# The rotary columns of latent attention: one 128-column product for the swapped queries, one pass for the key's two parts

## The chip, the cores and the metric

The program runs on one core of one Trainium2 chip. The metric is the time of one execution on the device in microseconds (us), first to last instruction and what lies around them. Smaller is better.

## What is computed

Two layers of a hybrid block over 256 latent tokens and 256 context tokens of width 1024: a modulated norm, one input projection, four parallel groups of token mixing, an output projection, and a mixture of 16 experts. The change lies in group D, the multi-head latent attention with rotary position parts:

```python
MLA_HEADS, MLA_Q_RANK, MLA_KV_RANK = 4, 256, 128
MLA_NOPE_DIM, MLA_ROPE_DIM = 64, 32

def rope_2d(x, cos, sin):
    r1, r2, c1, c2 = jnp.split(x, 4, axis=-1)
    x1 = jnp.concatenate([r1, c1], axis=-1)
    x2 = jnp.concatenate([r2, c2], axis=-1)
    o1 = x1 * cos - x2 * sin
    o2 = x1 * sin + x2 * cos
    ...

pl = modulate(rms_norm(xl, norm1_g[l]), mod_l[0], mod_l[1]) @ w_in[l]      # latent tokens; pc likewise for context
dl, dc = pl[..., OFF_D:], pc[..., OFF_D:]
q = (rms_norm(dl[..., :256], gq) @ w_uq).reshape(B, L, 4, 64 + 32)          # 64 plain, 32 rotary columns a head
k_rope = dl[..., 256 + 128:]                                                # 32 columns, shared by the heads
qr_l, kr_l = rope_2d(qr_l, cos, sin), rope_2d(kr_l, cos, sin)               # latent tokens only
```

A rotation is `x * cos + swapped(x) * sin`, where `swapped` exchanges the halves of each group of 16 columns and the sign stands in `sin`. The kernel takes the swapped vector from the same product as the vector itself, with a second copy of the weight columns in swapped order.

## The kernel before

Activations lie with their features on the 128 partitions and the tokens along a row: `x_t` is 8 chunks of 128 features by 512 tokens (256 latent, 256 context). A large product is done in three passes of TensorE: weights and activations are each split into a high and a low part (`w_hi`, `w_lo`, `h_hi`, `h_lo`), and `product` (L1177 to L1179) adds hi·hi, hi·lo and lo·hi into one PSUM bank. The split of a weight block is a copy on ACT (`w_hi`, L809) followed by a subtraction on DVE (`w_lo`, L1807).

The input projection of a layer runs over eight blocks of 256 weight columns, n = 0 to 7. `W_COLS = [6, 7, 5, 4, 0, 1, 2, 3]` says which columns each takes: n = 0 holds the low-rank query (`q_low`), n = 1 holds the low-rank key and value (128 columns, `kv_low`) and the 32 rotary key columns (`k_rope`), which GpSimd (POOL) follows with a swapped copy of them (`swap`, L664), so that the block is 192 columns wide. A block of features is a pass `by_feature(n, dst, c0, m, width)`: 8 chunks of 3 matmuls, with `m` weight columns from `c0` held still and `width` tokens streamed. After a block come two things in TensorE's program: a product of the modulation, `modulate(q, bank[7])` at L1206 in layer 0 after blocks 2 to 7 and in layer 1 after blocks 3 and 5, and `after_block(n)`, small products that the block before made possible. In the middle of the next block stands `turn(q, bank[7])` (L1214), which waits for `mod_row`, a row that DVE copies from `bank[7]` (`take_rows`, L1828).

For n = 1 TensorE does three passes: 128 columns by 512 tokens into `bank[2]` (`kv_low`), 96 columns by 512 tokens into `bank[3]`, and 96 columns by 256 latent tokens into `bank[4]`. The last two are 96 wide although only 32 columns of each are wanted, so that the rotary columns land on partitions 64 to 95 in the first and the swapped ones on the same partitions in the second. There DVE makes the key's rotation: L1946 (`k_rope`), L1947 (`k_turn`), L1948, L1951, all on `rr`, partitions 64 to 95.

For the queries GpSimd builds `w_uqs` in `small_weights` (L684, L688), each head's 96 columns with the last 32 swapped. After block 6, `after_block(6)` multiplies it: four heads by two chunks, 96 columns by 256 latent tokens each (L1352), two heads to a bank. In plain float32, each such product appears as two matmul records in the profile. Then comes `up_k(0, bank[4])` (L1312), the first half of the keys. DVE turns the result into `rope_t` with the sine (L1989), multiplies `q_mla` by the cosine (L1995) and adds (L1996); only after these, in layer 0, does it reach `take_rows(6)` (L1828), for whose `mod_row` the `turn(6)` inside block 7 waits.

All order is written out by hand: each engine has one program, and semaphores (`used`, `s_up`, `s_rot`, `s_mod`, `split_lo`) tie them. Weight blocks come through a ring of six 1 MB buffers `raw`, loaded in one order on SyncE's queue (SP). A buffer comes free when DVE has made `w_lo` from it, or, for modulation weights, when `modulate` has read it (L594, L535, L548).

Of the kernel before, what the change touches and what calls it, by code (L numbers as in the profile page):

```python
# [84 lines left out]
def constants():  # L85
# [20 lines left out]
    for part in range(2):  # L106
        for half in range(2):
            r = NOPE + part * 2 * nf + half * nf
            c[r:r + nf, C_COS:C_COS + S] = cos[part * nf:(part + 1) * nf]
            c[r:r + nf, C_SIN:C_SIN + S] = sin[part * nf:(part + 1) * nf] * (-1 if half == 0 else 1)  # L110
# [5 lines left out]
def build(nc, a, out):  # L116
    with ExitStack() as ctx:  # L117
# [42 lines left out]
        w_uqs = sb("w_uqs", [P, 2, HEADS, QK])  # L160
# [487 lines left out]
        def _(pool):  # L648
# [18 lines left out]
            def small_weights(l):  # L667
# [15 lines left out]
                for c in range(2):  # L683
                    pool.tensor_copy(w_uqs[:, c, :, 0:NOPE], w4[:, c, :, 0:NOPE])  # L684
                    for half in range(2):
                        for part in range(2):
                            to, fr = NOPE + 16 * part + 8 * half, NOPE + 16 * part + 8 * (1 - half)
                            last = pool.tensor_copy(w_uqs[:, c, :, to:to + 8], w4[:, c, :, fr:fr + 8])  # L688
# [93 lines left out]
        def _(act):  # L782
# [133 lines left out]
            for l in range(DEPTH):  # L916
# [13 lines left out]
                for n in range(N_WIN):  # L930
# [29 lines left out]
                    if n == 4:  # L960
                        for h in range(3):
                            act.wait_ge(s_up, l * 9 + h + 1)
                            act.activation(q_mla[0:QK, h, 0:width], bank[4 + h][0:QK, 0:width], ACT.Copy, scale=MLA_SCALE).then_inc(s_qe, 1)
                    if n == 5:
                        act.wait_ge(s_up, l * 9 + 4)
                        act.activation(q_mla[0:QK, 3, 0:width], bank[4][0:QK, 0:width], ACT.Copy, scale=MLA_SCALE).then_inc(s_qe, 1)
                    if n == 6:
                        act.wait_ge(s_up, l * 9 + 7)
                        act.activation(k_mla[0:NOPE, 0, :], bank[4][0:NOPE, :], ACT.Copy)
                        act.activation(k_mla[0:NOPE, 1, :], bank[4][NOPE:P, :], ACT.Copy).then_inc(s_ke, 1)  # L970
                    if n == 7:
                        act.activation(v_na[:, 0:2, :].rearrange("p t n -> p (t n)"), bank[2][:, :], ACT.Copy).then_inc(proj_ea, 1)
                        act.wait_ge(s_up, l * 9 + 8)
                        act.activation(k_mla[0:NOPE, 2, :], bank[4][0:NOPE, :], ACT.Copy)
                        act.activation(k_mla[0:NOPE, 3, :], bank[4][NOPE:P, :], ACT.Copy).then_inc(s_ke, 1)
                        act.wait_ge(s_up, l * 9 + 9)
# [197 lines left out]
        def _(pe):  # L1174
# [92 lines left out]
            for l in range(DEPTH):  # L1267
# [48 lines left out]
                def after_block(n, l=l):  # L1316
# [31 lines left out]
                    if n == 6:  # L1348
                        pe.wait_ge(s_go, l + 1)
                        for h in range(HEADS):  # L1350
                            for c in range(2):
                                ins = pe.matmul(bank[5 + h // 2][0:QK, (h % 2) * S:(h % 2 + 1) * S], w_uqs[:, c, h, :],  # L1352
                                                q_low[:, c, 0:S], start=(c == 0), stop=(c == 1))
                            if h % 2:
                                ins.then_inc(s_up, 1)
# [13 lines left out]
                for n in range(N_WIN):  # L1369
# [18 lines left out]
                    elif n == 1:  # L1388
                        by_feature(n, bank[2], 0, P, T)
                        by_feature(n, bank[3], 64, QK, T)  # L1390
                        ins = by_feature(n, bank[4], 96, QK, S)
# [400 lines left out]
        def _(dve):  # L1792
# [113 lines left out]
            for l in range(DEPTH):  # L1906
# [29 lines left out]
                for n in range(N_WIN):  # L1936
# [8 lines left out]
                    if n == 1:  # L1945
                        dve.tensor_copy(k_rope[rr, :], bank[3][rr, :])  # L1946
                        then(dve.tensor_tensor(k_turn[rr, :], bank[4][rr, 0:S], const[rr, C_SIN:C_SIN + S], ALU.mult))  # L1947
# [38 lines left out]
                    if n == 6:  # L1986
                        dve.wait_ge(s_up, l * 9 + 6)
                        for h2 in range(2):
                            ins = dve.scalar_tensor_tensor(rope_t[rr, 2 * h2:2 * h2 + 2, :], bank[5 + h2][rr, :].rearrange("p (h t) -> p h t", h=2),  # L1989
                                                           MLA_SCALE, const[rr, C_SIN:C_SIN + S][:, None, :].to_broadcast([ROPE, 2, S]),  # L1990
                                                           ALU.mult, ALU.mult)
# [387 lines left out]
```

## Time and profile before

| | |
|---|---|
| median of 3 executions | 944.04 us (940.52 to 949.8) |
| profiled execution | 942.83 us |
| its span, first to last instruction | 941.0 us |
| mean granted clock of TensorE | 0.935 of full speed |
| PE (matmul) busy | 853.3 us, 91% |
| DVE, ACT, POOL busy | 551.7, 463.5, 77.8 us |
| moved by DMA | 197.50 MB |

PE is TensorE's matmuls and PEld its weight loads. A matmul's duration overlaps the next one's, so what a matmul costs in a stream is the distance from its start to the next start. The input projection of layer 0 lies at about 50 to 189 us, that of layer 1 at about 575 to 669 us.

### The profile page before, as it was taken

Reading aid. Unit: us, or ns where it says so; the run is one execution under the profiler, and the core shown is the slowest. Engines: PE = TensorE matmul, PEld = TensorE weight load, DVE = VectorE, ACT = ScalarE, POOL = GpSimd, SP = SyncE. Lnnn points to the kernel's source line nnn. Section 1 sums busy time; section 2 is a strip of 40 time slices with the busy share of each in tenths; the row PEclk is TensorE's granted clock in tenths of the full one; section 3 lists DMA queues with packets and bytes.
Section 4 is the critical chain, followed back from the end, with each engine's and each line's share of the span. In section 5 each row is a group of like instructions: output and inputs, shape, how many; then the busy total and the mean of one; then the engine's idle time right before and its main releaser. Section 6 shows DMA issues by size and latency. Waiting matters only on the chain. (4 is left out here: it accounts for less than half of the span.)

```text
span 941.0 us, 15302 instructions
## 1 busy us (share of the span) xinstructions
PE 853.3 (91%) x6114; PEld 728.1 (77%) x6114; DVE 551.7 (59%) x800; ACT 463.5 (49%) x637; POOL 77.8 (8%) x107
## 2 busy tenths in 40 slices
PE   3989999999998889999999567999999799999986
PEld 2768867756786689999999466887769599999974
DVE  1263312349534868777777374434285678888853
ACT  2262211168523556655665337422384557776734
POOL 0103000610012000000000132002200100000000
PEclk9799999999999699999999756999999799999996
DMA  9793898793121157888888891279063249999901
GB/s 327 219 311 103 281 320 275 237 311 99 53 90 46 45 175 259 293 293 283 288 293 272 262 280 50 91 227 310 10 215 117 78 134 316 349 339 330 351 20 45
DMA packets 165443, 197.50 MB, mean 210 GB/s; under 512 B 11346, under 2 KB 152572, under 8 KB 165372
## 3 DMA queue, kind: packets, MB, share of 16 engines
q1 hardware_dynamic: 160720, 180.70, 60.2%
q10 hardware_dynamic: 3500, 11.64, 3.2%
q0 software_dynamic: 1152, 4.19, 1.3%
q8 instruction: 47, 0.77, 0.4%
q14 instruction: 24, 0.20, 0.1%
HBM read 187.09 MB, written 9.44 MB: 209 GB/s over the span
## 5 line engine op out<-in xcount | busy, mean ns | idle before, releaser
L2072 DVE TENSOR_TENSOR w_lo<-raw,w_hi 128x2048 fp32r<-128x2048 f32 x96 | 219.5, 2290 | 38.0 <-ACT w_hi L1034 37.4
L1034 ACT ACTIVATE w_hi<-raw 128x2048 fp32r<-128x2048 f32 x96 | 183.5, 1913 | 67.1 <-PE bank L1179 58.1
L1177 PE MATMUL bank<-h_hi,w_hi 128*128 128x512 f32 (+3 forms) x304 | 109.6, 360 | 12.5 <-DVE h_lo L1864 10.4
L1177 PE MATMUL bank<-w_hi,xg_hi 128*128 128x256 f32 x384 | 111.7, 291 | 2.9 <-DVE xg_lo L2233 2.4
L1178 PE MATMUL bank<-w_lo,xg_hi 128*128 128x256 f32 x384 | 109.3, 285 | 0.0
L1179 PE MATMUL bank<-w_hi,xg_lo 128*128 128x256 f32 x384 | 109.2, 284 | 0.0
L1178 PE MATMUL bank<-h_lo,w_hi 128*128 128x512 f32 (+3 forms) x304 | 106.2, 349 | 0.0
L1179 PE MATMUL bank<-h_hi,w_lo 128*128 128x512 f32 (+3 forms) x304 | 106.0, 349 | 0.0
L1177 PEld LDWEIGHTS bank<-w_hi,xg_hi 128*128 128x128 f32 x384 | 74.1, 193 | 3.2 <-issue 3.2
L1177 PEld LDWEIGHTS bank<-h_hi,w_hi 128*128 128x128 f32 (+1 forms) x304 | 57.6, 190 | 23.8 <-issue 9.5
L1178 PEld LDWEIGHTS bank<-w_lo,xg_hi 128*128 128x128 f32 x384 | 74.4, 194 | 0.0
L1179 PEld LDWEIGHTS bank<-w_hi,xg_lo 128*128 128x128 f32 x384 | 74.3, 193 | 0.0
L1807 DVE TENSOR_TENSOR w_lo<-raw,w_hi 128x2048 fp32r<-128x2048 f32 (+1 forms) x20 | 45.1, 2263 | 48.5 <-ACT w_hi L809 48.3
L809 ACT ACTIVATE w_hi<-raw 128x2048 fp32r<-128x2048 f32 (+1 forms) x20 | 37.2, 1867 | 72.1 <-PE bank L1179 26.2
L1596 PE MATMUL bank<-onehot,h_tok 128*128 128x256 f32 x512 | 64.5, 284 | 1.3 <-DVE onehot L2078 1.3
L1596 PEld LDWEIGHTS bank<-onehot,h_tok 128*128 128x128 f32 x512 | 63.5, 192 | 2.3 <-ACT h_tok L881 1.7
L1179 PEld LDWEIGHTS bank<-h_hi,w_lo 128*128 128x128 f32 (+1 forms) x304 | 57.8, 190 | 7.7
L1178 PEld LDWEIGHTS bank<-h_lo,w_hi 128*128 128x128 f32 (+1 forms) x304 | 57.8, 190 | 7.5 <-issue 0.2
L1177 PE MATMUL bank<-w_hi,ht_hi 128*128 128x512 f32 x128 | 52.8, 412 | 6.7 <-DVEq L2336 4.1
L1179 PE MATMUL bank<-w_hi,ht_lo 128*128 128x512 f32 x128 | 52.1, 407 | 0.0
L1178 PE MATMUL bank<-w_lo,ht_hi 128*128 128x512 f32 x128 | 52.0, 406 | 0.0
L1206 PE MATMUL bank<-raw,c_pad 128*32 128x256 f32 x768 | 45.8, 392 | 2.5 <-DMA raw<-in_ada_w 2.5
(292 smaller groups left out, 1619.7 us busy)
## 6 DMA issues: line engine op xcount, KB each, us to landing
raw<-in_ada_w SPq DMA_DIRECT2D x48, 1024.0 KB, 9.9
raw<-in_moe_w_gate SPq DMA_DIRECT2D x32, 1024.0 KB, 6.1
raw<-in_moe_w_up SPq DMA_DIRECT2D x32, 1024.0 KB, 6.5
raw<-in_moe_w_down SPq DMA_DIRECT2D x32, 1024.0 KB, 6.0
raw<-in_w_in SPq DMA_DIRECT2D x14, 1024.0 KB, 9.7
raw<-in_w_out SPq DMA_DIRECT2D x8, 1024.0 KB, 9.7
y_rows<-y_sb ACTq DMA_DIRECT2D x16, 512.0 KB, 5.0
na_bias<-in_na_rpb SPq DMA_DIRECT2D x4, 384.0 KB, 8.3
```

The lines of the kernel that those rows point to most:

```text
L809: act.activation(w_hi[slot][:, :, 0:w], raw[n % RAW][:, :, 0:w], ACT.Copy).then_inc(split_hi, 1)
L1034: act.activation(w_hi[slot][:, :, :], raw[q][:, :, :], ACT.Copy).then_inc(split_hi, 1)
L1177: pe.matmul(dst, w_hi_, x_hi_, start=first, stop=False)
L1178: pe.matmul(dst, w_hi_, x_lo_, start=False, stop=False)
L1179: return pe.matmul(dst, w_lo_, x_hi_, start=False, stop=last)
L1206: ins = pe.matmul(dst[32 * g:32 * g + 32, 0:BW], c_pad[:, k, :], raw[raw_index(l, j) % RAW][:, k, :], start=(k == 0), stop=(k == KC - 1))
L1596: ins = pe.matmul(bank[c // 2][:, (c % 2) * 2 * SLOTS:(c % 2 + 1) * 2 * SLOTS], h_tok[part][:, t, c * P:(c + 1) * P], onehot[:, t, :], sta ...
L1807: dve.tensor_tensor(w_lo[slot][:, :, 0:w], raw[n % RAW][:, :, 0:w], w_hi[slot][:, :, 0:w].bitcast(F32), ALU.subtract).then_inc(split_lo, 1)
L2072: dve.tensor_tensor(w_lo[slot][:, :, :], raw[q][:, :, :], w_hi[slot][:, :, :].bitcast(F32), ALU.subtract).then_inc(split_lo, 1)
```

## The change

The constants `cos` and `sin`, which lay on partitions 64 to 95, are repeated on all four groups of 32 partitions. `w_uqs` keeps only the 32 swapped columns of each head, so that four heads make one stationary operand of 128 columns: `after_block(6)` does one product of two chunks into `bank[5]`, with head h on partitions 32h to 32h+31. DVE then makes `rope_t` in four instructions, one a head, each reading another group of partitions of `bank[5]` and of the sine, and writing partitions 64 to 95. GpSimd no longer copies the plain columns. For n = 1 the two 96-column passes become one pass of 64 columns by 512 tokens into `bank[3]`: rotary columns on partitions 0 to 31, swapped on 32 to 63. DVE reads them there and writes partitions 64 to 95. The counts of `s_up` fall from 9 to 8 a layer. Nothing else is touched.

```diff
@@ constants()
-    for part in range(2):
+    for part in range(2 * P // ROPE):
         for half in range(2):
-            r = NOPE + part * 2 * nf + half * nf
-            c[r:r + nf, C_COS:C_COS + S] = cos[part * nf:(part + 1) * nf]
...
+            r = part * 2 * nf + half * nf
+            c[r:r + nf, C_COS:C_COS + S] = cos[part % 2 * nf:(part % 2 + 1) * nf]
...
-        w_uqs = sb("w_uqs", [P, 2, HEADS, QK])
+        w_uqs = sb("w_uqs", [P, 2, HEADS, ROPE])
@@ small_weights, GpSimd
                 for c in range(2):
-                    pool.tensor_copy(w_uqs[:, c, :, 0:NOPE], w4[:, c, :, 0:NOPE])
                     for half in range(2):
                         for part in range(2):
-                            to, fr = NOPE + 16 * part + 8 * half, NOPE + 16 * part + 8 * (1 - half)
+                            to, fr = 16 * part + 8 * half, NOPE + 16 * part + 8 * (1 - half)
                             last = pool.tensor_copy(w_uqs[:, c, :, to:to + 8], w4[:, c, :, fr:fr + 8])
@@ after_block, TensorE
                     if n == 6:
                         pe.wait_ge(s_go, l + 1)
-                        for h in range(HEADS):
-                            for c in range(2):
-                                ins = pe.matmul(bank[5 + h // 2][0:QK, (h % 2) * S:(h % 2 + 1) * S], w_uqs[:, c, h, :],
-                                                q_low[:, c, 0:S], start=(c == 0), stop=(c == 1))
-                            if h % 2:
-                                ins.then_inc(s_up, 1)
+                        for c in range(2):
+                            ins = pe.matmul(bank[5][:, 0:S], w_uqs[:, c, :, :].rearrange("p h r -> p (h r)"), q_low[:, c, 0:S],
+                                            start=(c == 0), stop=(c == 1))
+                        ins.then_inc(s_up, 1)
@@ block n == 1, TensorE
                         by_feature(n, bank[2], 0, P, T)
-                        by_feature(n, bank[3], 64, QK, T)
-                        ins = by_feature(n, bank[4], 96, QK, S)
+                        ins = by_feature(n, bank[3], P, 2 * ROPE, T)
@@ block n == 1, DVE
-                        dve.tensor_copy(k_rope[rr, :], bank[3][rr, :])
-                        then(dve.tensor_tensor(k_turn[rr, :], bank[4][rr, 0:S], const[rr, C_SIN:C_SIN + S], ALU.mult))
+                        dve.tensor_copy(k_rope[rr, :], bank[3][0:ROPE, :])
+                        then(dve.tensor_tensor(k_turn[rr, :], bank[3][ROPE:2 * ROPE, 0:S], const[ROPE:2 * ROPE, C_SIN:C_SIN + S], ALU.mult))
@@ block n == 6, DVE
-                        dve.wait_ge(s_up, l * 9 + 6)
-                        for h2 in range(2):
-                            ins = dve.scalar_tensor_tensor(rope_t[rr, 2 * h2:2 * h2 + 2, :], bank[5 + h2][rr, :].rearrange("p (h t) -> p h t", h=2),
-                                                           MLA_SCALE, const[rr, C_SIN:C_SIN + S][:, None, :].to_broadcast([ROPE, 2, S]),
+                        dve.wait_ge(s_up, l * 8 + 5)
+                        for h in range(HEADS):
+                            hr = slice(ROPE * h, ROPE * h + ROPE)
+                            ins = dve.scalar_tensor_tensor(rope_t[rr, h, :], bank[5][hr, 0:S], MLA_SCALE, const[hr, C_SIN:C_SIN + S],
                                                            ALU.mult, ALU.mult)
```

TensorE's program in layer 0 from the end of `modulate` after block 6 into block 7, before (here `w_uqs` is the swapped query weight, `kv_low` with `w_ukv` is `up_k(0)`, and the L1299 to L1301 rows are block 7):

```order
L1206 MATMUL bank<-raw_56,c_pad 32x256
L1352 MATMUL bank<-q_low,w_uqs 96x256 x8
L1312 MATMUL bank<-kv_low,w_ukv 64x512 x2
L1299 MATMUL bank<-w_hi_58,h_hi 128x256
L1300 MATMUL bank<-w_lo_61,h_hi 128x256
```

And the same place in the changed kernel:

```order
L1205 MATMUL bank<-raw_56,c_pad 32x256
L1350 MATMUL bank<-q_low,w_uqs 128x256 x2
L1311 MATMUL bank<-kv_low,w_ukv 64x512 x2
L1298 MATMUL bank<-w_hi_58,h_hi 128x256
L1299 MATMUL bank<-w_lo_61,h_hi 128x256
```

Eight matmul instructions have become two, and nothing around them has moved.

DVE's program at the same time, from `w_lo` of block 7 to the rows of the modulation, before:

```order
L1807 TENSOR_TENSOR w_lo_61<-raw_57,w_hi_58 128x2048
L1989 SCALAR_TENSOR_TENSOR rope_t<-bank,const 32x512 x2
L1995 TENSOR_TENSOR q_mla<-q_mla,const 32x4x256
L1996 TENSOR_TENSOR q_mla<-q_mla,rope_t 32x4x256
L1828 COPY mod_row<-bank 128x256
```

And in the changed kernel:

```order
L1803 TENSOR_TENSOR w_lo_61<-raw_57,w_hi_58 128x2048
L1986 SCALAR_TENSOR_TENSOR rope_t<-bank,const 32x256 x4
L1991 TENSOR_TENSOR q_mla<-q_mla,const 32x4x256
L1992 TENSOR_TENSOR q_mla<-q_mla,rope_t 32x4x256
L1824 COPY mod_row<-bank 128x256
```

Two instructions of 512 elements a partition are four of 256; the order stays. In block 1, TensorE's 48 matmuls of 96 columns (24 of them by 512 tokens, 24 by 256) become 24 of 64 columns by 512 tokens in the same place, and DVE's four instructions keep their order.

## Rows read from the trace of the kernel before

**Rows 1.** The page: its first line.

```profile
span 941.0 us, 15302 instructions
```

**Rows 2.** Waits of PE from 60 to 250 us: total us, times, longest.

```profile
PE bank L1214 <- DVE mod_row L1828: 2.4, 2, 1.5
...
PE bank L1206 <- DMA raw<-in_ada_w: 1.1, 1, 1.1
```

**Rows 3.** Waits of PE from 560 to 670 us.

```profile
PE bank L1177 <- DVE w_lo L1807: 1.2, 1, 1.2
```

**Rows 4.** PE in time, block 1 of layer 0: start us, us, instruction.

```profile
68.55 0.39 PE L1177 MATMUL bank<-h_hi,w_hi 128*96 128x512 f32 x1
...
74.07 0.28 PE L1177 MATMUL bank<-h_hi,w_hi 128*96 128x256 f32 x1
...
76.92 0.28 PE L1299 MATMUL bank<-w_hi,h_hi 128*128 128x256 f32 x1
```

**Rows 5.** PE in time, block 1 of layer 1.

```profile
598.21 0.28 PE L1177 MATMUL bank<-h_hi,w_hi 128*96 128x256 f32 x1
...
601.06 0.28 PE L1299 MATMUL bank<-w_hi,h_hi 128*128 128x256 f32 x1
```

**Rows 6.** PE in time, layer 0, after block 6 and into block 7.

```profile
167.20 3.69 PE L1352 MATMUL bank<-q_low,w_uqs 128*96 128x256 f32 x16
170.82 1.08 PE L1312 MATMUL bank<-kv_low,w_ukv 128*64 128x512 f32 x4
171.83 0.39 PE L1299 MATMUL bank<-w_hi,h_hi 128*128 128x256 f32 x1
...
174.68 0.28 PE L1301 MATMUL bank<-w_hi,h_lo 128*128 128x256 f32 x1
176.41 0.44 PE L1214 MATMUL bank<-const,mod_row 128*128 128x128 f32 x2 [1.45 <-DVE mod_row L1828]
```

**Rows 7.** DVE in time, layer 0, the same stretch.

```profile
165.89 2.29 DVE L1807 TENSOR_TENSOR w_lo<-raw,w_hi 128x2048 fp32r<-128x2048 f32 x1 [0.81 <-ACT w_hi L809]
170.93 1.29 DVE L1989 SCALAR_TENSOR_TENSOR rope_t<-bank,const 32x512 f32<-32x512 f32 x2 [2.75 <-PE bank L1352]
172.33 1.54 DVE L1995 TENSOR_TENSOR q_mla<-q_mla,const 32x1024 f32<-32x1024 f32 x1
173.90 2.00 DVE L1996 TENSOR_TENSOR q_mla<-q_mla,rope_t 32x1024 f32<-32x1024 f32 x1
175.93 0.42 DVE L1828 COPY mod_row<-bank 128x256 f32<-128x256 f32 x1
```

**Rows 8.** By tile, `k_turn` and `rope_t`: duration ns min/median/max.

```profile
L1947 DVE TENSOR_TENSOR k_turn<-bank,const x1: 422/422/422, 77.8 to 77.8; 32x256 f32<-32x256 f32 x1
L1989 DVE SCALAR_TENSOR_TENSOR rope_t<-bank,const x2: 678/684/689, 170.9 to 171.5; 32x512 f32<-32x512 f32 x2
```

**Rows 9.** PE in time, layer 1, after block 6.

```profile
652.97 3.62 PE L1352 MATMUL bank<-q_low,w_uqs 128*96 128x256 f32 x16
656.52 1.08 PE L1312 MATMUL bank<-kv_low,w_ukv 128*64 128x512 f32 x4
```

**Rows 10.** DVE in time, layer 1, the same two operations as in layer 0.

```profile
658.02 1.25 DVE L1995 TENSOR_TENSOR q_mla<-q_mla,const 32x1024 f32<-32x1024 f32 x1
659.30 1.54 DVE L1996 TENSOR_TENSOR q_mla<-q_mla,rope_t 32x1024 f32<-32x1024 f32 x1
```

**Rows 11.** Stretches of layer 0: length, busy of five engines, clock, DMA share, GB/s.

```profile
109.00:111.00 2.00, 2.00 (x44) 1.23 (x40) 0.00 (x0) 2.00 (x3) 0.00 (x0) 1.00 0.05 15
147.00:149.00 2.00, 2.00 (x37) 1.07 (x30) 0.65 (x1) 1.22 (x1) 0.00 (x0) 1.00 0.00 0
184.00:190.00 6.00, 6.00 (x81) 3.45 (x79) 1.11 (x2) 0.60 (x1) 4.13 (x4) 1.00 0.02 7
```

**Rows 12.** PE in time, layer 0, and the stretch behind it (columns as in rows 11).

```profile
305.05 0.66 PE L1577 MATMUL bank<-const,nh 128*128 128x128 f32 x4 [2.24 <-ACT nh L890]
306.00:309.00 3.00, 2.27 (x9) 1.48 (x9) 2.76 (x10) 3.00 (x7) 0.00 (x0) 0.50 0.00 0
```

More of the change, by code:

```diff
@@ L105, in constants @@
     cos, sin = np.cos(ang).T, np.sin(ang).T
-    for part in range(2):
+    for part in range(2 * P // ROPE):
         for half in range(2):
-            r = NOPE + part * 2 * nf + half * nf
-            c[r:r + nf, C_COS:C_COS + S] = cos[part * nf:(part + 1) * nf]
-            c[r:r + nf, C_SIN:C_SIN + S] = sin[part * nf:(part + 1) * nf] * (-1 if half == 0 else 1)
+            r = part * 2 * nf + half * nf
+            c[r:r + nf, C_COS:C_COS + S] = cos[part % 2 * nf:(part % 2 + 1) * nf]
+            c[r:r + nf, C_SIN:C_SIN + S] = sin[part % 2 * nf:(part % 2 + 1) * nf] * (-1 if half == 0 else 1)
     c[:, C_RANK:C_RANK + 64] = np.tile(np.array([3, 2, 1, 0], np.float32), 16)
@@ L961, in _ @@
                         for h in range(3):
-                            act.wait_ge(s_up, l * 9 + h + 1)
+                            act.wait_ge(s_up, l * 8 + h + 1)
                             act.activation(q_mla[0:QK, h, 0:width], bank[4 + h][0:QK, 0:width], ACT.Copy, scale=MLA_SCALE).then_inc(s_qe, 1)
                     if n == 5:
-                        act.wait_ge(s_up, l * 9 + 4)
+                        act.wait_ge(s_up, l * 8 + 4)
                         act.activation(q_mla[0:QK, 3, 0:width], bank[4][0:QK, 0:width], ACT.Copy, scale=MLA_SCALE).then_inc(s_qe, 1)
                     if n == 6:
-                        act.wait_ge(s_up, l * 9 + 7)
+                        act.wait_ge(s_up, l * 8 + 6)
                         act.activation(k_mla[0:NOPE, 0, :], bank[4][0:NOPE, :], ACT.Copy)
@@ L972, in _ @@
                         act.activation(v_na[:, 0:2, :].rearrange("p t n -> p (t n)"), bank[2][:, :], ACT.Copy).then_inc(proj_ea, 1)
-                        act.wait_ge(s_up, l * 9 + 8)
+                        act.wait_ge(s_up, l * 8 + 7)
                         act.activation(k_mla[0:NOPE, 2, :], bank[4][0:NOPE, :], ACT.Copy)
                         act.activation(k_mla[0:NOPE, 3, :], bank[4][NOPE:P, :], ACT.Copy).then_inc(s_ke, 1)
-                        act.wait_ge(s_up, l * 9 + 9)
+                        act.wait_ge(s_up, l * 8 + 8)
                         act.activation(v_mla[:, 0:2, :].rearrange("p t n -> p (t n)"), bank[5][:, :], ACT.Copy)
```

## The prediction

> **What bounds the kernel now.** The profiled execution took 942.83 us, of which 941.0 are its span [rows 1]. I read first what TensorE (PE) waits for in the two projection stages, since every matmul that the change touches lies there, and PE is busy for 91% of the span. From 60 to 250 us of layer 0 the view of waits has two waits that matter here: 2.4 us in two pieces on `mod_row`, the longer 1.5 us, and 1.1 us on a modulation weight still in flight [rows 2]. In layer 1 the only long one inside the blocks is 1.2 us on `w_lo` [rows 3]. So PE sets the pace in both stages, and a matmul taken from its program there brings the next one forward, as long as nothing that PE waits for keeps its old time. The rest of the reading asks that question of each wait: is it counted from something that itself moves forward?
>
> For loads it is. DMA stands still in layer 0 before every product of the modulation: share 0.05 at 109 to 111 us, 0.00 at 147 to 149, 0.02 at 184 to 190 [rows 11], because the ring is full and the next loads are issued only when PE has read the old ones. They start with PE and keep their distance to it. The 1.1 us on `raw` is of this kind (the loads were issued when `modulate` after block 7 had freed their buffers), and so is the 1.2 us on `w_lo` in layer 1: that block's load stands in the queue behind four modulation blocks which wait for the product after block 3, and block 3 comes earlier by all that is saved in block 1.
>
> **Block 1 (n = 1), twice.** Before, three passes; the last one, 24 matmuls of 96 columns by 256 tokens, runs in layer 0 from 74.07 to 76.92 us [rows 4] and in layer 1 from 598.21 to 601.06 [rows 5]. Both are 2.85 us, 0.119 a matmul, with no gap before the next block. This pass goes. The other pass keeps its 24 matmuls of 512 tokens and becomes 64 columns wide instead of 96: (74.07 − 68.55) / 24 = 0.230 us each [rows 4]. What a stream of 64-column matmuls costs no row shows for these operands. I take the same 0.230, since what is streamed is the same 512 tokens. The bound above is the nearest 64-column row, the float32 product of `up_k`: (171.83 − 170.82) / 4 = 0.2525 us a record [rows 6], which would cost 24 × 0.0225 = 0.54 us a layer, 1.1 in all. Below, 0.213 us is what 512 columns take at 2.4 GHz, a gain of 0.4 a layer, 0.8 in all. DVE's four instructions for the key keep their number and sizes; they now read partitions 0 to 63 and write 64 to 95. Nobody on the path waits for them: the next thing on DVE is `w_lo` of block 3, and it is block 2 that PE does meanwhile. GpSimd's two fewer copies a layer end before any of PE's waits on `s_wg` and are worth nothing. The cover there is blocks 2 and 3; without it they would be a small gain, not a cost.
> Sum: −2.85 in layer 0 and −2.85 in layer 1.
>
> **After block 6, layer 1.** The swapped queries are 8 instructions, 16 records, from 652.97 to 656.52 us [rows 9]: 3.55 us, 0.222 a record. Two instructions, 4 records, stay. A record streams 256 columns whether 96 or 128 are held, so I take the same price: 12 × 0.222 = 2.66 us less. DVE's work with the result is not waited for before the attention scores of this group, which stand behind block 7 and the first attention jobs; the `turn` inside block 7 exists in layer 0 only. In layer 1 PE therefore keeps all of it: −2.66. Were a 128-column record dearer, at the 0.2525 of `up_k`, the four would cost 0.12 more.
>
> **After block 6, layer 0.** Here 12 × (170.82 − 167.20) / 16 = 2.71 us leave PE's program [rows 6], but PE meets a wait soon after: at 174.96 it has done the first part of block 7 and stands for 1.45 us, until `turn(6)` at 176.41, on `mod_row` [rows 6]. `mod_row` is copied by DVE at 175.93, behind `rope_t` and two operations on `q_mla` [rows 7]. So this part is worth what DVE's chain gains, not what PE's does. `rope_t` starts when PE has finished the product, at 170.93; 2.71 earlier is 168.22. DVE is free just then: `w_lo` of block 7 ends at 165.89 + 2.29 = 168.18. Before, the two instructions and the step to L1995 take 172.33 − 170.93 = 1.40 us, 1.29 of it the pair [rows 7]. After, there are four of 32 partitions by 256 elements. The row of that size and with the same kinds of operands (PSUM and a constant) is `k_turn`, 0.422 us [rows 8]: 4 × 0.422 = 1.69, 0.40 more than the pair. The copy of `mod_row` comes 2.71 − 0.40 = 2.31 us earlier, and so does all of PE after `turn(6)`; PE's wait there becomes 1.45 + 0.40 = 1.85. The matmuls removed save 2.71, and 0.40 of it turns into a longer wait.
>
> The two rows before overlap a little: 2 × 0.684 = 1.37 us of durations lie in 1.29 us [rows 7, 8], 0.08 for the joint. With the same overlap four would take 4 × 0.422 − 3 × 0.08 = 1.45, and this part would be −2.55, the whole −10.91. I take the sum without overlap, because each of the four reads another group of partitions than the one before, which the pair did not. The Trainium skill says so as a rule, on the page "VectorE: DVE Perf Modes", section "Two Vector instructions with no wait between them": an instruction whose input starts in another group of 32 partitions than the last read of that memory is held until all earlier ones have finished. No row of this trace tests it.
>
> The two operations on `q_mla` (1.54 and 2.00 us) lie beside GpSimd's window sums; in layer 1 the same two took 1.25 and 1.54 [rows 7, 10]. Started 2.3 us earlier against a GpSimd that has not moved, they may take from 0.75 less to about 0.5 more. I leave them as they are. A queue that is passed over is none here: no instruction changes its place, SP's queue and GpSimd's included.
>
> **Sum:** 2.85 + 2.31 + 2.85 + 2.66 = 10.67 us less. Span 930.3, execution 932.2. The median of the runs shown is 944.04, 1.2 above the profiled execution, so I expect 944.04 − 10.7 = **933.4 us**, −1.13%. The bounds of the unknown prices give −8.9 (64 columns dear, 128 dear, `q_mla` slower) to −12.5 (64 columns cheap, overlap, `q_mla` faster).
>
> **Rivals.**
> 1. *The loads of layer 0 hold their time.* Between the pauses of rows 11 DMA is at work. If its stream rather than PE sets the stage, the 5.2 us of layer 0 turn into waits of `modulate` on `raw`, and 5.5 remain: 938.5. For it: the 1.1 us on `raw` [rows 2]. Against it: the pauses of 2 to 6 us before each product [rows 11], which a stream that sets the pace would not have. Chance 0.08.
> 2. *The gain is given back behind the stage.* Attention and experts run on PE, DVE and ACT close together, and DVE's wait for a weight or a clock that returns later could eat a part; half of it would be −5.3, 938.7. For it: norms between stages stand at half clock, and how long differs from place to place [rows 12]. Against: nothing there is tied to a time that does not move. 0.16, and the same play to the other side widens the range below.
> 3. *The clock falls inside block 7, and the kernel is slower.* PE's wait at `turn(6)` grows to 1.85 us. In this trace PE worked at 1.2 GHz at 306 to 309 us, after a wait of 2.24 us [rows 12]; the wait of 1.45 us left the clock at its full level: block 7's matmuls behind it are as short as before it [rows 6, 11]. Each us of dense work at the lower level loses half a us, so 21.3 us of it eat 10.67, which is the point from which it decides; 40 us, about to the middle of the attention, lose 20 and give 944.04 − 10.7 + 20 = 953.4. Against it: from 176 us on PE has dense work again at once. 0.03.
> 4. *The change does not do what it says:* the order of instructions has two products for eight, so only the width could disappoint: if the 64-column pass cost as much as the two it replaces, 5.7 would be missing: 939.1. Nothing but the 0.2525 points there. 0.03.
> The forecast itself holds 0.70.
>
> **How the numbers follow.** Medians of this kernel spread from 940.5 to 949.8, so about 1%, 9.4 us, is what a measurement of it can tell from no change; the forecast lies only 1.2 us beyond. Of its 0.70 I put 0.58 below 934.6 and the rest, with rivals 1, 2 and 4, within 1%: faster 0.58, same 0.39, slower 0.03. The range: bounds −12.5 to −8.9 and 2.5 us for the medians on the fast side, 928.5; on the slow side it takes in rivals 1 and 2, 939.5.
>
> **What would show it.** In the changed profile: in block 1 of both layers 24 matmuls of 64 columns at 0.230 us, block 2 starting 2.85 us earlier; four records of L1350 in about 0.9 us; four `rope_t` of 0.42 in 1.69 us; a wait before `turn(6)` of about 1.85 us; in layer 1 the wait on `w_lo` before block 6 still 1.2 us; block 6 of layer 1 starting 8.0 us (2.85 + 2.31 + 2.85) early and block 7 10.7. I am wrong if DMA's pauses shrink and the waits on `raw` grow, if `mod_row` comes less than 2 us earlier within its stage, or if the stages after 250 us take another time than before.

## The result and the profile after

| | before | after |
|---|---|---|
| median of the executions | 945.02 us (940.52 to 949.8, 4 runs) | 933.04 us (932.35 to 934.72, 4 runs) |
| profiled execution | 942.83 us | 933.12 us |
| span | 941.0 us | 931.3 us |

The ratio is 0.9862, with a 95% interval from 0.9833 to 0.9891. The forecast was 933.4 us and a ratio of 0.989. The total is right. One of its four terms is not: layer 0 behind block 6 gave nothing in this profile, and stretches that the change does not touch made up for it.

The page of the changed kernel, its first lines (busy us, share of the span, instructions):

```profile
span 931.3 us, 15158 instructions
...
PE 841.8 (90%) x6042; PEld 717.3 (77%) x6042; DVE 552.3 (59%) x804; ACT 463.6 (50%) x637; POOL 78.3 (8%) x103
```

**Block 1.** PE in time, block 1 of layer 0 and the beginning of block 2 (answers to [rows 4]), then layer 1 ([rows 5]):

```profile
67.21 0.40 PE L1176 MATMUL bank<-h_hi,w_hi 128*64 128x512 f32 x1
67.45 0.39 PE L1177 MATMUL bank<-h_lo,w_hi 128*64 128x512 f32 x1
...
72.73 0.28 PE L1298 MATMUL bank<-w_hi,h_hi 128*128 128x256 f32 x1
...
590.46 0.40 PE L1176 MATMUL bank<-h_hi,w_hi 128*64 128x512 f32 x1
...
595.98 0.28 PE L1298 MATMUL bank<-w_hi,h_hi 128*128 128x256 f32 x1
```

24 matmuls of 64 columns take 5.52 us in both layers, 0.230 each, as the 96-column ones did. The pass of 2.85 us behind them is gone, and block 2 follows at once.

**Behind block 6, layer 0.** First PE (answers to [rows 6]):

```profile
163.04 1.13 PE L1350 MATMUL bank<-q_low,w_uqs 128*128 128x256 f32 x4
164.10 1.08 PE L1311 MATMUL bank<-kv_low,w_ukv 128*64 128x512 f32 x4
...
168.05 0.28 PE L1300 MATMUL bank<-w_hi,h_lo 128*128 128x256 f32 x1
171.03 0.61 PE L1213 MATMUL bank<-const,mod_row 128*128 128x128 f32 x2 [2.71 <-DVE mod_row L1824]
...
171.66 0.42 PE L1299 MATMUL bank<-w_lo,h_hi 128*128 128x256 f32 x1
171.87 0.41 PE L1300 MATMUL bank<-w_hi,h_lo 128*128 128x256 f32 x1
```

The product is four records in 1.06 us instead of sixteen in 3.62. But the wait before `turn(6)` has grown from 1.45 us to 2.71, where 1.85 was forecast, and behind it the matmuls stand 0.21 us apart instead of 0.12. That is the granted clock, as three stretches show: the wait, what follows it, and after that (length; busy us of PE, PEld, DVE, ACT, POOL; clock; share of DMA; GB/s).

```profile
168.10:170.90 2.80, 0.23 (x2) 0.02 (x1) 2.73 (x3) 0.00 (x0) 2.72 (x2) 1.00 1.10 350
171.30:174.30 3.00, 3.00 (x16) 3.00 (x15) 0.24 (x2) 0.00 (x0) 2.77 (x4) 0.50 1.10 349
174.60:177.00 2.40, 2.40 (x22) 2.40 (x21) 0.00 (x0) 0.00 (x0) 0.38 (x1) 1.00 1.10 348
```

TensorE worked at 1.2 GHz from `turn(6)` to about 174.5 us and at 2.4 GHz again behind that. DVE, the same stretch (answers to [rows 7]):

```profile
162.24 2.91 DVE L1803 TENSOR_TENSOR w_lo<-raw,w_hi 128x2048 fp32r<-128x2048 f32 x1 [1.32 <-ACT w_hi L808]
165.18 1.72 DVE L1986 SCALAR_TENSOR_TENSOR rope_t<-bank,const 32x256 f32<-32x256 f32 x4
167.00 1.31 DVE L1991 TENSOR_TENSOR q_mla<-q_mla,const 32x1024 f32<-32x1024 f32 x1
168.35 2.17 DVE L1992 TENSOR_TENSOR q_mla<-q_mla,rope_t 32x1024 f32<-32x1024 f32 x1
170.55 0.42 DVE L1824 COPY mod_row<-bank 128x256 f32<-128x256 f32 x1
```

The four sine instructions take 1.72 us (forecast 1.69). They start at 165.18, though the product was done by 164.10 or little later, because `w_lo` ended only at 165.15. There are two reasons. It began later: 2.79 us behind the start of `modulate` after block 6 (162.24 − 159.45), against 2.28 before (165.89 − 163.61), because the copy `w_hi` ahead of it, on ACT, waited longer for block 7's weight. Before, then after:

```profile
163.94 1.92 ACT L809 ACTIVATE w_hi<-raw 128x2048 fp32r<-128x2048 f32 x1 [12.53 <-DMA raw<-in_w_in]
```

```profile
160.29 1.91 ACT L808 ACTIVATE w_hi<-raw 128x2048 fp32r<-128x2048 f32 x1 [13.04 <-DMA raw<-in_w_in]
```

And it took 2.91 us and not 2.29. What stands beside it is GpSimd's program, the window sums, which no row ahead of the prediction shows. Before:

```profile
163.85 2.14 POOL L708 TENSOR_TENSOR win_a<-a_pad 128x542 f32<-128x542 f32 x2 [82.72 <-PE bank L1179]
166.07 4.21 POOL L708 TENSOR_TENSOR win_b<-win_a 64x538 f32<-64x538 f32 x2
170.36 1.07 POOL L708 TENSOR_TENSOR win_a<-win_b 128x530 f32<-128x530 f32 x1
171.51 1.27 POOL L708 TENSOR_TENSOR win_b<-win_a 64x512 f32<-64x512 f32 x1
```

And after:

```profile
159.70 2.14 POOL L707 TENSOR_TENSOR win_a<-a_pad 128x542 f32<-128x542 f32 x2 [80.19 <-PE bank L1178]
161.91 4.17 POOL L707 TENSOR_TENSOR win_b<-win_a 64x538 f32<-64x538 f32 x2
166.16 1.08 POOL L707 TENSOR_TENSOR win_a<-win_b 128x530 f32<-128x530 f32 x1
167.32 2.12 POOL L707 TENSOR_TENSOR win_b<-win_a 64x512 f32<-64x512 f32 x1
```

GpSimd begins when PE has finished block 6, in both kernels. The pair `win_b` takes 4.2 us in both. The difference is who came first: before, `w_lo` (165.89) began 0.18 us ahead of the pair (166.07) and took 2.29; after, it began 0.33 us behind it (162.24 against 161.91) and took 0.62 more. The last line, 1.27 us before and 2.12 after, lies beside `q_mla`. The experiments below test this.

**Layer 1.** PE in time ([rows 9] before): the same two products, with no wait behind them.

```profile
647.54 1.02 PE L1350 MATMUL bank<-q_low,w_uqs 128*128 128x256 f32 x4
648.50 1.08 PE L1311 MATMUL bank<-kv_low,w_ukv 128*64 128x512 f32 x4
```

The product takes 0.96 us instead of 3.55. The wait on `w_lo` before block 6 ([rows 3], 1.2 us) is 0.87:

```profile
636.25 0.50 PE L1176 MATMUL bank<-h_hi,w_hi 128*128 128x512 f32 x1 [0.87 <-DVE w_lo L1803]
```

**The balance along the span.** The start of the same PE instruction in both traces, in us:

| place | before | after | shift | of this |
|---|---|---|---|---|
| `turn` before block 1, layer 0 | 45.43 | 44.10 | −1.33 | not forecast |
| `modulate` at 84 us, behind block 1 | 88.53 | 84.34 | −4.19 | block 1: −2.86 |
| `up_k(0)` | 170.82 | 164.10 | −6.72 | product: −2.53 |
| `turn(6)` | 176.41 | 171.03 | −5.38 | longer wait: +1.34 |
| `modulate` after block 7 | 185.41 | 181.54 | −3.87 | clock: +1.51 |
| first norm row behind the experts | 551.42 | 549.20 | −2.22 | given back: +1.65 |
| `up_k(0)` of layer 1 | 656.52 | 648.50 | −8.02 | block 1 −2.87, product −2.63, wait −0.30 |
| final norm | 927.85 | 918.16 | −9.69 | gained besides: −1.67 |

The 1.33 us at the start lie in the first norm and the first product of the modulation, ahead of every product that the change touches. The queries' part alone shows 1.3 us of the same sign there, the kernel before with another order of DVE (experiment 4) 0.4 of the other. Two profiles of one kernel differ by as much: this `turn` starts at 44.12 and 45.83 us in the two of the queries' part alone, at 44.11 and 45.80 in the two with the rows first (experiments 4 and 6). So I count it as variation between executions. Nine of the eleven profiles with the change or a part of it have 44.1 to 44.3, the two with neither part 45.4 and 45.9; whether the change alters how often the short start comes is not shown.

### The profile page after: what moved, and what is told of

Same layout as the page of the kernel before. It is cut to its first block and busy times, and to the rows that moved or that the text cites. A ratio compares the mean times of both kernels' runs of the same rounds, so it can differ in the third digit from the quotient of the medians.

```text
span 931.3 us, 15158 instructions
## 1 busy us (share of the span) xinstructions
PE 841.8 (90%) x6042; PEld 717.3 (77%) x6042; DVE 552.3 (59%) x804; ACT 463.6 (50%) x637; POOL 78.3 (8%) x103
## 3 DMA queue, kind: packets, MB, share of 16 engines
q0 software_dynamic: 1152, 4.19, 1.4%
## 5 line engine op out<-in xcount | busy, mean ns | idle before, releaser
L1176 PE MATMUL bank<-h_hi,w_hi 128*128 128x512 f32 (+2 forms) x288 | 105.4, 366 | 12.0 <-DVE h_lo L1860 10.1
L1177 PE MATMUL bank<-h_lo,w_hi 128*128 128x512 f32 (+2 forms) x288 | 101.6, 353 | 0.0
L1178 PE MATMUL bank<-h_hi,w_lo 128*128 128x512 f32 (+2 forms) x288 | 101.5, 353 | 0.0
L1803 DVE TENSOR_TENSOR w_lo<-raw,w_hi 128x2048 fp32r<-128x2048 f32 (+1 forms) x20 | 45.4, 2277 | 54.1 <-ACT w_hi L808 54.0
L1176 PEld LDWEIGHTS bank<-h_hi,w_hi 128*128 128x128 f32 (+1 forms) x288 | 54.7, 190 | 23.5 <-issue 9.5
L1178 PEld LDWEIGHTS bank<-h_hi,w_lo 128*128 128x128 f32 (+1 forms) x288 | 54.8, 190 | 8.2
L1177 PEld LDWEIGHTS bank<-h_lo,w_hi 128*128 128x128 f32 (+1 forms) x288 | 54.9, 191 | 7.7 <-issue 0.2
L1205 PE MATMUL bank<-raw,c_pad 128*32 128x256 f32 x768 | 45.4, 390 | 1.3 <-DMA raw<-in_ada_w 1.3
```

The costliest lines, as they stand in the source:

```text
L1176: pe.matmul(dst, w_hi_, x_hi_, start=first, stop=False)
L1177: pe.matmul(dst, w_hi_, x_lo_, start=False, stop=False)
L1178: return pe.matmul(dst, w_lo_, x_hi_, start=False, stop=last)
L1205: ins = pe.matmul(dst[32 * g:32 * g + 32, 0:BW], c_pad[:, k, :], raw[raw_index(l, j) % RAW][:, k, :], start=(k == 0), stop=(k == KC - 1))
L1803: dve.tensor_tensor(w_lo[slot][:, :, 0:w], raw[n % RAW][:, :, 0:w], w_hi[slot][:, :, 0:w].bitcast(F32), ALU.subtract).then_inc(split_lo, 1)
```

## The experiments

Times before in the comparisons below: 945.49 us (25 runs, the first group), 945.83 (11, the second), 946.19 (11, the third).

**1. Each part alone.** The key's part alone:

```diff
-                        by_feature(n, bank[3], 64, QK, T)
-                        ins = by_feature(n, bank[4], 96, QK, S)
+                        ins = by_feature(n, bank[3], P, 2 * ROPE, T)
```

with DVE's two reads and the constants as in the change, and the query product as before.

> The key's part alone: block 1 in one 64-column pass instead of two of 96, the swapped queries as before. Theory A (what was forecast, term by term): each layer's block 1 is 2.86 us shorter and nothing takes it back, 5.7 us in all, about 938.5 to 939.5 against a median before of 945.0; block 2 of both layers starts 2.85 us earlier counted from the start of block 1, and the wait before the turn inside block 7 of layer 0 stays at 1.45 us with the clock at full level. Rival B (the 9.7 us of the changed kernel come mostly from elsewhere, a start that happened to be 1.3 us shorter and clock phases): less than 3 us in the stages, the rest scattered.

Measured: 940.95 us, ratio 0.9946 [0.9928, 0.9965]. The median lies 1.5 us above what was expected. Block 1 gives 2.85 us in each layer, and the wait before `turn(6)` is 1.42 us. `w_lo` of block 7 took 2.97 us here too, with no harm: the long product ends later, and DVE still idles 1.63 us before the rotation. The queries' part alone is the rest of the diff:

> The queries' part alone: two products of 128 columns instead of eight of 96, four sine instructions, the key as before. Theory A': the product is 2.5 to 2.7 us shorter in both layers, but only layer 1 keeps it; in layer 0 the wait for the modulation's rows behind it grows from 1.45 to about 2.7 us because DVE starts the sine only after its weight split, and PE comes back at 1.2 GHz for some 3 us (about 1.5 us lost), so nothing or up to 0.5 us is left there: 2.5 to 3 us in all, about 942. Rival (the forecast's term for layer 0): 2.3 us kept in layer 0 too, 5.0 in all, about 940, with a wait near 1.85 us and no fall of the clock.

Measured: 938.63 us, ratio 0.9924 [0.9894, 0.9955]. In layer 1 the product gives 2.63 us, whole; in layer 0 it gives 2.6, of which the wait before `turn(6)`, now 2.69 us, takes 1.34 back. The median lies 3.4 us below the expected 942: the wait grew as expected, but the clock did not fall in this profile. The two ratios multiply to 0.987, the whole change within its interval; that the parts add up fits, but the intervals are too wide to show it. A second profile of this kernel:

> A second profile of the queries' part alone. In its first the wait before turn(6) was 2.69 us and the clock stayed at 1.00 behind it. If that wait length alone decided, it stays again; if it is chance at such lengths, either may be seen. The weight split before the rotation takes over 2.5 us beside GpSimd's sums.

Its wait is again 2.71 us, and this time the clock falls: at 175.5 us, still in the wait, and it stays at 1.2 GHz until 182.3, 6.0 us of dense matmuls, which cost 2.6 us (from `turn(6)` to `modulate` after block 7 it is 11.63 us, against 8.98 in the first profile). The single execution took 944.23 us, the slowest single one of any changed kernel. It lies behind its first profile by 4.4 us at `modulate` after block 7 and by 8 to 10 at the end, so it says nothing of the part's worth; it shows how far single executions scatter.

**2. The price of reading another partition group each time.** All four instructions read partitions 0 to 31. The kernel then computes something else, since heads 1 to 3 take head 0's rotary part, but the sizes stay:

```diff
-                            ins = dve.scalar_tensor_tensor(rope_t[rr, h, :], bank[5][hr, 0:S], MLA_SCALE, const[hr, C_SIN:C_SIN + S],
+                            ins = dve.scalar_tensor_tensor(rope_t[rr, h, :], bank[5][0:ROPE, 0:S], MLA_SCALE, const[0:ROPE, C_SIN:C_SIN + S],
```

> The changed kernel, but the four sine instructions all read partitions 0 to 31 of the bank and of the sine, so that heads 1 to 3 take head 0's rotary part (the result is changed by that, the sizes are not). Theory (each is held back until the last has finished because it reads another group of partitions): the four shrink from 1.72 us to about 4 x 0.42 - 3 x 0.08 = 1.45. Rival (the order of partition groups is free): 1.7 as before. The wait in block 7 of layer 0 otherwise stays near 2.5 us, which also shows whether the clock falls behind such a wait every time.

DVE and GpSimd in time:

```profile
162.44 2.88 DVE L1803 TENSOR_TENSOR w_lo<-raw,w_hi 128x2048 fp32r<-128x2048 f32 x1 [1.34 <-ACT w_hi L808]
165.35 1.41 DVE L1986 SCALAR_TENSOR_TENSOR rope_t<-bank,const 32x256 f32<-32x256 f32 x4
166.87 1.62 DVE L1991 TENSOR_TENSOR q_mla<-q_mla,const 32x1024 f32<-32x1024 f32 x1
168.53 2.17 DVE L1992 TENSOR_TENSOR q_mla<-q_mla,rope_t 32x1024 f32<-32x1024 f32 x1
170.73 0.42 DVE L1824 COPY mod_row<-bank 128x256 f32<-128x256 f32 x1
...
159.87 2.14 POOL L707 TENSOR_TENSOR win_a<-a_pad 128x542 f32<-128x542 f32 x2 [78.20 <-PE bank L1178]
162.09 4.17 POOL L707 TENSOR_TENSOR win_b<-win_a 64x538 f32<-64x538 f32 x2
166.34 1.08 POOL L707 TENSOR_TENSOR win_a<-win_b 128x530 f32<-128x530 f32 x1
```

The execution took 932.98 us. The four take 1.41 us instead of 1.72: 0.10 for each of the three joints, close to the 0.08 that the prediction took from the pair of before. The rule of the Trainium skill that it cited for held instructions ("VectorE: DVE Perf Modes", "Two Vector instructions with no wait between them") agrees: with the same group each time they overlap, with another they don't. But `mod_row` is not copied earlier. The next instruction, which reads two operands from SBUF, takes 1.62 us instead of 1.31 and uses the 0.31 up. Counted from GpSimd's start, the copy comes 10.86 us later here (170.73 − 159.87) and 10.85 in the changed kernel (170.55 − 159.70). The wait before `turn(6)` is 2.71 us in both. So a shorter rotation does not shorten the chain: the instruction behind it, which reads SBUF twice beside GpSimd's sums, ends at the same distance from their start (8.62 and 8.61 us).

**3. GpSimd out of the way.** Its window sums wait for the rotation, and nothing else is changed:

```diff
                 pool.wait_ge(used, done(l, N_ADA + 6))
+                pool.wait_ge(s_rot, l * 2 + 2)
```

> The changed kernel with GpSimd's window sums held back until DVE has made the query's rotation. Theory: GpSimd's work beside it is what stretches DVE's weight split of block 7 in layer 0 to 2.9 us and the two operations on q_mla to 1.3 and 2.2; without it the split takes 2.29, the two 1.25 and 1.54 or less, and the wait in block 7 falls from 2.71 to between 1.3 and 1.6 us, with the clock at full level. Rival: the split's length comes from the traffic of the loads; it stays near 2.9 and the wait above 2.2.

DVE in time, and PE at `turn(6)`:

```profile
163.31 2.29 DVE L1804 TENSOR_TENSOR w_lo<-raw,w_hi 128x2048 fp32r<-128x2048 f32 x1 [1.47 <-ACT w_hi L809]
165.64 1.73 DVE L1987 SCALAR_TENSOR_TENSOR rope_t<-bank,const 32x256 f32<-32x256 f32 x4
167.47 1.22 DVE L1992 TENSOR_TENSOR q_mla<-q_mla,const 32x1024 f32<-32x1024 f32 x1
168.72 1.22 DVE L1993 TENSOR_TENSOR q_mla<-q_mla,rope_t 32x1024 f32<-32x1024 f32 x1
...
170.45 0.44 PE L1214 MATMUL bank<-const,mod_row 128*128 128x128 f32 x2 [1.27 <-DVE mod_row L1825]
```

`w_lo` is back at 2.29 us and `q_mla` takes 2.44 instead of 3.48; the rotation, which reads PSUM and one operand of SBUF, is unmoved at 1.73. GpSimd's pair `win_b`, now behind the rotation, takes 2.24 us instead of 4.17. The wait is 1.27 us, at the lower edge of the 1.3 to 1.6 expected, and the clock stays at 1.00.

From the start of `modulate` after block 6 to `turn(6)` it is 10.07 us (170.45 − 160.38), against 11.58 in the changed kernel (171.03 − 159.45) and 12.80 before (176.41 − 163.61); the forecast's 2.31 would have made it 10.49. Holding GpSimd back gives 1.51 us, more than the 1.09 that was lost. But the forecast's term does not simply come back. The sine starts 5.26 us behind `modulate` where the forecast had 4.61 (168.22 − 163.61), because `w_lo` again begins late, at 2.93 instead of 2.28; and the two operations on `q_mla` take 2.44 us where the forecast kept 3.54. The two differences, 0.65 and 1.10, have opposite signs.

(The whole execution took 939.16 us. By the same instructions it lay 2.1 us ahead of the changed kernel at 181 us, 2.7 at 302 and 2.0 at 741, 1.1 behind at 758 and 6.0 behind at 918. The clock explains the losses in part: 0.50 at 746 to 750 us and 0.64 at 750 to 756, against 0.75 and 1.00 in the changed kernel, and 0.56 against 0.63 from 905 to 931. It is one execution; I draw nothing from its total.)

How `w_lo` and the pair `win_b` meet is the same in all profiles in which GpSimd works there. The end of `w_lo`, counted from the pair's start:

| kernel | `w_lo` starts after the pair | takes | sum |
|---|---|---|---|
| before | −0.18 | 2.29 | |
| before, rows first | 0.06 | 3.18 | 3.24 |
| rows first, twice | 0.22, 0.16 | 3.01, 3.07 | 3.23, 3.23 |
| changed, twice | 0.33, 0.37 | 2.91, 2.86 | 3.24, 3.23 |
| queries alone, twice | 0.61, 0.20 | 2.63, 3.03 | 3.24, 3.23 |
| key alone | 0.26 | 2.97 | 3.23 |
| one group; wide pass | 0.35, 0.25 | 2.88, 2.98 | 3.23, 3.23 |

Begun 0.06 to 0.61 us behind the pair, `w_lo` ends 3.23 us after the pair began, as if it stood still until 0.94 us behind the pair's start, most of one GpSimd instruction (1.12 us with DVE out of the way), and then took its 2.29. The first two rows are of one program up to this place: in the second execution `w_lo` began 0.24 us later against the pair and took 3.18 us, so the 2.29 that the forecast read was a matter of the execution. The Trainium skill has this as a rule, on the page "SBUF — State Buffer", section "Who interferes with whom": DVE and GpSimd share a pair of ports, a DVE operation with both inputs in SBUF contends for it with a GpSimd operation that reads SBUF, and whichever issues first keeps it for the whole instruction. The table agrees, and so do the unmoved rotation and the two operations on `q_mla`.

Which of the two comes first hangs on block 7's weight. GpSimd's first sum starts 0.24 or 0.25 us behind `modulate` wherever it is not held back. `w_hi`, which waits for the weight, starts 0.33 and 0.58 us behind `modulate` in the two profiles with the old products, and 0.68 to 1.11 in the eleven others. Why the weight comes later there, no run separates.

**4. The rows first.** If the wait on `mod_row` is the loss, the copy can go ahead of the rotation, right behind `w_lo`:

```diff
                     if n == 6:
+                        if n in AFTER_BLOCK[l]:
+                            take_rows(AFTER_BLOCK[l][n], bank[7])
                         dve.wait_ge(s_up, l * 8 + 5)
```

> The changed kernel with one copy moved: after block 6 DVE copies the modulation's rows before it makes the query's rotation, not after it. Theory: the wait inside block 7 of layer 0 (2.71 us in the changed kernel) goes, and with it the fall of the clock behind it (1.5 us), so block 7 ends about 4.2 us earlier counted from the product after block 6: about 929, ratio to before near 0.982. Rival (the loads hold their time): the next modulation product waits for its weights instead, the wait on raw grows from 1.1 us by 3 or more, and the time stays at 932 to 933.

Measured: 930.76 us, ratio 0.9843 [0.9814, 0.9873]. DVE in time, and PE at `turn(6)`:

```profile
163.00 3.01 DVE L1803 TENSOR_TENSOR w_lo<-raw,w_hi 128x2048 fp32r<-128x2048 f32 x1 [1.22 <-ACT w_hi L808]
165.93 0.41 DVE L1824 COPY mod_row<-bank 128x256 f32<-128x256 f32 x1
...
169.04 0.38 PE L1213 MATMUL bank<-const,mod_row 128*128 128x128 f32 x2
```

No wait is left, and the clock stays at 1.00. Against the changed kernel, `turn(6)` comes 2.9 us sooner within the stage and the end of block 7 4.4, of which 1.5 are the clock. The stage does what was expected; the median is 1.8 us above the expected 929. The same edit on the kernel before:

> The kernel before with the same copy moved ahead of the rotation, nothing else. Theory: its wait of 1.45 us inside block 7 of layer 0 goes, there was no fall of the clock behind it, so 1.4 us less, about 943.5, within what can be measured; the stage shows it. Rival (loads hold their time): the 1.4 us return as a wait on raw before the next modulation product or in the attention behind it.

Measured: 943.23 us, ratio 0.9983 [0.9961, 1.0005]; 1.6 us gained in the stage, and no difference in the whole that can be told. Rows first and GpSimd held back together:

> Both edits: the modulation's rows copied ahead of the rotation, and GpSimd's window sums held back behind it. Theory: with the rows first nothing waits for the rotation, and the weight split of block 7, which ended just as TensorE came for it, ends 0.6 us before; so no more than 0.1 us over the kernel with the rows first alone, 930 to 931, the same within what can be measured. Rival: GpSimd's sums, 3 to 6 us later, now end too late for the attention or the output projection, and the time goes up by 1 to 3 us.

Measured: 933.86 us, ratio 0.9871 [0.984, 0.9902]. In the stage nothing is left for a freer DVE to give: `modulate` after block 7 starts 17.58 us behind the one after block 6, against 17.67 with the rows first alone. The median lies 3 us above the expected 930 to 931, where the rival had put it; the intervals of the two kernels overlap, and that GpSimd's later sums cost something behind the stage is neither shown nor excluded.

**5. The width of the key's pass.** 128 columns instead of 64, 64 of them unused:

```diff
-                        ins = by_feature(n, bank[3], P, 2 * ROPE, T)
+                        ins = by_feature(n, bank[3], 64, P, T)
```

> The changed kernel with the pass for the key 128 columns wide instead of 64 (columns 64 to 191), read by DVE from partitions 64 to 95 and 96 to 127. Theory: a pass costs by the tokens it streams, not by the columns it holds, so its 24 matmuls take 0.227 to 0.230 us each as at 64 columns, and DVE's copy and product stay at 0.68 and 0.42 us whether they change partitions or not. Rival: width costs, and each takes over 0.24.

PE in time:

```profile
67.25 0.39 PE L1176 MATMUL bank<-h_hi,w_hi 128*128 128x512 f32 x1
...
72.69 0.28 PE L1298 MATMUL bank<-w_hi,h_hi 128*128 128x256 f32 x1
```

The pass takes 5.44 us, 0.227 each, 0.08 us less than with 64 columns; the execution took 932.11 us. With 64, 96 and 128 columns held the cost is 0.230, 0.230 and 0.227 us: it is the 512 tokens streamed that count here, not the columns.

**6. Once more: the clock, and rows first against the change.**

> The changed kernel once more, with a second profile. If the clock follows from the wait of 2.7 us before turn(6), this profile shows the wait at 2.6 to 2.8 us and a granted clock of 0.5 in at least one stretch of 2 us between 170 and 176 us, as three of four such waits did. If the fall was chance, the clock stays 1.00 there, as it did once, and the stage ends about 1.5 us earlier. Time 932 to 934 us.

Measured: 932.79 us, ratio 0.9874 [0.9852, 0.9896]. The wait is 2.70 us again, and the clock does not fall: the length of the wait alone does not decide it. The window of 3 us behind `turn(6)`, here and then in the second profile of the queries' part alone:

```profile
172.27:175.27 3.00, 3.00 (x28) 3.00 (x27) 0.24 (x2) 0.00 (x0) 2.76 (x4) 1.00 1.10 349
```

```profile
176.63:179.63 3.00, 3.00 (x16) 3.00 (x15) 0.24 (x2) 0.00 (x0) 2.77 (x4) 0.50 1.10 349
```

28 matmuls in one, 16 in the other, with waits of 2.70 and 2.71 us. Of the six profiles with such a wait, four fell (changed, one group, wide pass, queries alone the second time) and two did not; with waits of 1.27 to 1.45 us (before, key alone, GpSimd held back) none of three fell. In three of the four it fell when the matmuls had begun again and came back after 3.4 us, in the fourth during the wait, for 6.8 us.

> The copy of the rows ahead of the rotation, against the changed kernel on the same chip. By the stage's own shifts it is 4.5 us faster than the changed kernel: 928.5 to 930. If what a stage gains is given back behind it, the two are within 1.5 us of each other. No wait before turn(6) over 0.5 us, clock 1.00 from 166 to 176 us.

Measured: 931.93 us, ratio 0.9856 [0.9834, 0.9878], 0.9 us below the changed kernel on the same chip; the first time it was 2.3 below, against another group's runs. In the stage the gain is there (`turn(6)` 2.9 us sooner, counted from the end of block 6; the changed kernel kept its clock in this pair), but the medians differ by less than their intervals. It is the best version found, and its lead over the change is not shown beyond the stage.

## Why the prediction came out right, point by point

**Block 1, −2.85 twice.** Measured −2.86 and −2.87 in the changed kernel. The key's part alone brought the median from 945.49 to 940.95, 4.5 us less against 5.7 forecast; its interval, 3.3 to 6.8 us, takes that in. That 64 columns cost what 96 did is measured, and rival 4 with its dearer width is out.

**After block 6, layer 1, −2.66.** Measured −2.6. The four records take 0.24 us each, a little over the 0.222 taken.

**After block 6, layer 0, −2.31: this step failed.** The reading that PE's saving counts only as far as DVE's chain follows was right, and so was the price of the four sine instructions (1.72 against 1.69, the sum without overlap). Wrong was the step "DVE is free just then: `w_lo` of block 7 ends at 165.89 + 2.29 = 168.18". It left 0.04 us before the product's end at 168.22, took both the start and the duration of `w_lo` from one execution, and put no bound on either. In the changed kernel `rope_t` starts 5.73 us behind `modulate` (165.18 − 159.45) and not 4.61: 1.1 us later. Of this 0.51 is the later start of `w_lo`, with the arrival of block 7's weight, and 0.62 its duration, 2.91 us beside GpSimd's pair instead of 2.29. The duration had hung on `w_lo` having begun 0.18 us ahead of that pair. The prediction also took GpSimd as not moving, though its sums start with the end of block 6 and move with PE, and it took the loads as keeping their distance to PE, which this one kept only within half a microsecond.

From GpSimd's start to `turn(6)` it was 12.56 us before (163.85 to 176.41) and 11.33 after (159.70 to 171.03), −1.23; all six profiles with the new query product, GpSimd beside it and the old order of DVE have 11.33 to 11.35. In the profile shown the clock took another 1.5, and the term was worth +0.3; in the second profile it kept the −1.2. By the prediction's own sign, `mod_row` less than 2 us earlier within its stage, it was wrong here: the copy came 1.23 us earlier (10.85 us behind GpSimd's start against 12.08).

**Rival 3, the clock inside block 7,** was right in its place and wrong in its price. The wait came to 2.7 us and not 1.85, the clock fell in four of six profiles, and it stayed down for 3.4 us in three of them and 6.8 in one, not the 40 that the rival asked for: 1.5 us lost, and 2.6 in the one.

**Rival 1, loads that hold their time,** did not come about as a limit of the stage: the wait on `raw` in layer 0 stays at 1.1 us, and the wait on `w_lo` in layer 1 shrank by 0.3. **Rival 2, the gain given back behind the stage,** does not show in the sum: between layer 0's projection and layer 1's 1.65 us were given back, behind layer 1's 1.67 were gained. The two profiles of the queries' part alone differ by more, so neither can be put down to the change.

**The sum.** By the table, the change's own terms are 2.86 − 0.32 + 2.87 + 0.30 + 2.63 = 8.34 us, against 10.67 forecast. With the clock kept up, as in the second profile, 1.2 stand in place of the −0.32, and the sum is 9.9. The missing 0.8 to 2.3 are the failed step and the clock behind it, 1.1 to 2.6, less the 0.3 on `w_lo` in layer 1 that was not forecast. Block 6 of layer 1, forecast to start 8.0 us early, starts 5.4 early, and block 7's place there, forecast at 10.7, 8.0. The span shows 9.7: 1.33 more from the start, and 1.65 given back against 1.67 gained elsewhere. The medians differ by more, 11.0 from the median of before that the forecast started from (944.04), 12.0 and 13.4 within the two comparisons. Part of that is the profile of before, with 942.83 us a good execution of a kernel whose medians are 944 to 946. So the time was met by luck: 0.8 to 2.3 us are missing from the change's own terms, and from the forecast's starting point of 944.04 another 1.1 to 2.7 us (11.0 − 9.9, 11.0 − 8.34) lie in no stage of the change, up to 3.7 against the other medians. What these are stays open; the queries' part alone has them too (6.9 us in the medians, 3.9 by its terms of 2.6 and 1.3).

## What to carry to other kernels

A duration read from a trace holds only with its neighbours. Where an operation of DVE with two SBUF operands lies beside a GpSimd instruction, read which of the two began first, by how little, and whether the change or another execution alters that; ask also of the "other" engine what starts it, since here it was the same event that moves with the saving. And when TensorE's program gets shorter in front of a wait for another engine, look at what that engine does between the product and the copy TensorE waits for: the copy moved ahead of the unneeded rest gave 2.9 to 4.4 us in its stage, more than the 2.31 that had been forecast for it; in the medians its lead over the change is not shown.

## What was new of the hardware

- `w_lo` on DVE, beside GpSimd's pair `win_b`, ended 3.23 to 3.24 us after the pair's start in ten profiles, wherever between 0.06 and 0.61 us behind it it began; begun first (one profile), or with GpSimd held back (two), it took 2.29.
- Shortening the rotation by 0.31 us did not bring the copy behind it forward: it came 10.85 and 10.86 us after GpSimd's start.
- Another partition group read than by the instruction before cost DVE about 0.10 us each time (1.72 against 1.41 us for four).
- Around a wait of 2.69 to 2.71 us TensorE's clock fell to 1.2 GHz in four profiles of six, for 3.4 us in three (1.5 us lost) and 6.8 in one (2.6 lost); with waits of 1.27 to 1.45 us in none of three. The changed kernel and the queries' part alone each did both.
- A pass of 24 matmuls over 512 tokens costs 5.52 us with 64 or 96 columns held and 5.44 with 128.
